# Up projection of the second MLP: three 256-column products per weight tile instead of one of 512 and one of 256 columns

## The chip, the cores and the metric

The kernel runs on one core of a Trainium2 chip. The metric is the device time of one execution in microseconds; the time quoted for a kernel is the median of its runs. A trace of one execution, taken by the hardware profiler, stands beside the times.

## The reference, cut to what matters

The reference is a two-layer trunk (a recurrent block beside windowed attention in the first layer, a state-space layer with a gated projection in the second), with a squared-ReLU MLP behind each layer. The sequence has 256 frames, the model 2048 channels, the hidden layer of an MLP 8192. The change touches the MLP of the second layer:

```python
h = rmsnorm(x, ffn_norm[layer])
x = x + jnp.square(jax.nn.relu(h @ w_up[layer])) @ w_down[layer]
```

All data is float32.

## The kernel before, in words

**Two parts of each number.** TensorE multiplies in fp32r, which keeps fewer bits than float32. The kernel therefore splits each operand into a high part (rounded to fp32r) and a low part (the rest, rounded again), and a product A·W is summed from three: high·high, low·high and high·low. For the up projection the normalized input stands in the tile `A1` with channels on the partitions: `A1[:, k, 0:L]` is the high part of channel block k (L = 256 frames) and `A1[:, k, L:2*L]` its low part. One product with the high part of a weight tile as the stationary operand and all 512 columns of `A1[:, k, :]` as the moving one gives A_high·W_high in columns 0 to 255 of a PSUM bank and A_low·W_high in columns 256 to 511; a second one, with the low part of the weight tile and the 256 columns of the high part of the input, adds A_high·W_low to columns 0 to 255. Every product instruction comes with a weight load of its own 128x128 stationary operand.

**Staging of the second MLP.** The hidden layer is done in 8 rounds (`NE`, index `e`) of 1024 hidden channels. A round has an up stage of 4 pairs (`NPAIR`, index `j`) of 128-channel output blocks (index `t`). A pair contracts 16 channel blocks, held in 4 weight slots (index `s`) of 4 blocks each (index `c`). That makes 8 x 4 x 4 x 2 x 4 = 1024 weight tiles of 128x128, one 512-column product (L1258) and one 256-column product (L1259) for each. A pair fills two of the four `ps` banks, and pairs take turns in them. Then a round multiplies its hidden channels with the down weights: in rounds 0 to 6 two plain blocks (`second_block`, L1270 to L1272) and two groups of seven products on sums of quadrants (`seven_products`, L1311 to L1313), in the last round four plain blocks; their products all have 512 columns. The order of the work is the order of each engine's program; semaphores link the engines.

**The weights' way.** A weight slot comes by DMA into `raws`, ScalarE rounds it to the high part (L1730), VectorE takes the difference as the low part (L2292), and TensorE frees the slot with `slot_used`. A ring of 7 slots serves up and down weights alike.

**After a pair.** ScalarE copies columns 256 to 511 of the two banks to `cross` (`up_cross`, L1753), VectorE adds columns 0 to 255 to it (L2338, which then frees the banks with `up_read`), and applies the ReLU and the frames' scale (L2340, `scaled_up`). ScalarE squares (L1759) and rounds (L1761), VectorE makes the low parts (L2352) and the sums of quadrants for the seven products. These steps stand between the slots' rounding steps at the fixed places 4j+9 to 4j+11 of a round's slots.

**Opening.** The first four weight tiles of some pairs (the first pair of rounds 1 to 7, the pairs 1 to 3 of round 0) are multiplied in another order by `opening` (L828 with 512 columns, L826 with 256), which the first MLP uses as well. In form 3 the widths follow as 512, 256, 512, 512, 256, 256, 512, 256.

Of the kernel before, what the change touches and what calls it, by code (L numbers as in the profile page):

```python
# [28 lines left out]
ACT = mybir.ActivationFunctionType  # L29
ALU = mybir.AluOpType  # L30
AX = mybir.AxisListType

P = 128
D = 2048
L = 256
KC = D // P
# [12 lines left out]
UK = 4  # L49
# [17 lines left out]
NE = 8  # L67
NPAIR = 4
# [9 lines left out]
E_SLOTS = S_SLOT + QUADS * NPR  # L78
# [76 lines left out]
def trunk_kernel(nc, x, mix_norm_e, w_in_e, conv_w, conv_b, lru_wa, lru_ba, lru_wx, lru_bx, lru_lambda,  # L155
# [4 lines left out]
    with ctx:  # L160
        def sb(name, shape, dt=F32, on=ctx):
            return on.enter_context(nc.sbuf_tensor(name, shape, dt))

        def sem(name):
            return ctx.enter_context(nc.semaphore(name))
# [10 lines left out]
        A1 = sb("A1", [P, KC, 2 * L], F32R)  # L176
# [12 lines left out]
        Wh = sb("Wh", [P, NU, UK, TW], F32R)  # L189
        with ExitStack() as o:  # L190
            Wt = sb("Wt", [P, NU, UK * TW], on=o)
        Wl = sb("Wl", [P, NU, UK, TW], F32R)
# [47 lines left out]
        cross = sb("cross", [P, 2, 2, L])  # L240
# [35 lines left out]
        ps = ctx.enter_context(nc.psum_tensor("ps", [P, 4, 512], F32))  # L276
# [113 lines left out]
        slot_lo = sem("slot_lo")  # L390
        slot_used = sem("slot_used")
        t_summed = sem("t_summed")
        up_crossed = sem("up_crossed")
        up_read = sem("up_read")
        hid_done = sem("hid_done")
        scaled_up = sem("scaled_up")
        sx_done = sem("sx_done")
        a_hi = sem("a_hi")
        s_hi = sem("s_hi")
        a_done = sem("a_done")  # L400
        s_done = sem("s_done")
# [70 lines left out]
        def out_unit(u):  # L472

            return (u // 4, NU + u % 4) if u < 4 * NU else (u // 4 - NU, u % 4)

        def out_banks(b):

            return ps[:, 2 - 2 * b:4 - 2 * b, :] if b < 2 else px[:, 2 * b - 4:2 * b - 2, :]
# [17 lines left out]
        def sum_bank(n):  # L496

            return px[:, 0 if n in (2, 3) else 3, 0:L]
# [5 lines left out]
        def wide(t, s):  # L504

            return t[:, s].rearrange("p (k a) n -> p k (a n)", k=2)
# [32 lines left out]
        def in_tiles(ap, n):  # L539

            return ap.rearrange("p (c n) -> p c n", n=n)
# [29 lines left out]
        def gain(col):  # L571

            return pcol[:, bass.ds(col, 1)]
# [184 lines left out]
        def _(pe):  # L758
            mm = nc.tensor.matmul
# [56 lines left out]
                    for u in range(NU, 2 * NU):  # L816
                        products(u, 1).then_inc(unit_done, 1)

            def opening(form, b, A, high=Wh[:, 0], low_=Wl[:, 0]):

                order = {1: ((0, 0), (0, 1), (1, 1), (1, 0), (2, 0), (2, 1), (3, 0), (3, 1)),
                         2: ((0, 0), (1, 0), (0, 1), (1, 1), (2, 0), (2, 1), (3, 0), (3, 1)),
                         3: ((0, 0), (0, 1), (1, 0), (2, 0), (1, 1), (2, 1), (3, 0), (3, 1))}[form]
                for c, low in order:
                    if low:
                        mm(ps[:, b, 0:L], low_[:, c, 0:P], A[:, c, 0:L], start=False, stop=False)  # L826
                    else:
                        mm(ps[:, b, :], high[:, c, 0:P], A[:, c, :], start=(c == 0), stop=False)  # L828

            def pair(g, d, A, ready=None, base=0, per_unit=0, turn=0, beside=None, freed=None, form=None):  # L830

# [57 lines left out]
            for a in range(2):  # L889
                last = mm(sum_bank(1)[:, bass.ts(a, P)], ones[:, :], sq[:, a, 0:P], start=True, stop=True)  # L890
# [124 lines left out]
            for u in range(8 * NU):  # L1015
                b, n = out_unit(u)
# [10 lines left out]
                for h in range(2):  # L1027
                    for c in range(2):
                        k = 2 * n + c
                        high = A2[:, k, h * P:h * P + P]  # L1030
                        low = A2[:, k, L + h * P:L + h * P + P]
                        to = out_banks(b)[:, h, :]
                        mm(to, high, wide(Wh, u % NU)[:, c], start=(k == LC), stop=False)
                        mm(to, high, wide(Wl, u % NU)[:, c], start=False, stop=False)
                        last = mm(to, low, wide(Wh, u % NU)[:, c], start=False, stop=(k == LC - 1))
# [129 lines left out]
            for h in range(2):  # L1165
                n = NC4 // 2
                last = mm(sum_bank(3)[:, h * n:h * n + n], pos4[:, :], sq[:, h, 0:n], start=True, stop=True)
# [61 lines left out]
            def last_block(s):  # L1229

                if s == 1:
                    turn_back(3, px, x_glu, 8)
                if s == 2:
                    frame_sum(4, 6)

            def second_up(e, j):

                b = 2 * (j % 2)
                if j >= 2:
                    pe.wait_ge(up_read, e * NPAIR + j - 1)  # L1240
                elif e:
                    pe.wait_ge(acc_read, (e - 1) * NPR + 2 * j + 2)
                else:
                    pe.wait_ge(pair_read, P_MLP1 - 4)
                form = 3 if e and j == 0 else j if e == 0 and 1 <= j <= 3 else None
                for s in range(NU):
                    p = e * E_SLOTS + j * UK + s
                    high, low = [in_tiles(v, TW) for v in slot_parts(p)[0:2]]
                    pe.wait_ge(slot_lo, p + 1)
                    if e == 0 and j == 0:  # L1250
                        pe.wait_ge(a1_ready, 16 + 2 * (s + 1))
                    if form and s == 0:
                        opening(form, b, A1, high, low)
                    for t in range(1 if form and s == 0 else 0, 2):
                        for c in range(UK):
                            k = s * UK + c
                            cols = slice(t * P, t * P + P)
                            mm(ps[:, b + t, :], high[:, c, cols], A1[:, k, :], start=(k == 0), stop=False)  # L1258
                            last = mm(ps[:, b + t, 0:L], low[:, c, cols], A1[:, k, 0:L], start=False, stop=(k == KC - 1))  # L1259
                    last.then_inc(slot_used, 1)  # L1260
                    if e == 0 and j == 0:
                        last_block(s)
# [67 lines left out]
        def _(act):  # L1330
            fn = nc.scalar.activation
# [65 lines left out]
            for i in range(KC // 2):  # L1397
                act.wait_ge(xt_done, i + 1)
                src = px[:, i % 3, :].rearrange("p (c t) -> p c t", c=2)
                for c in range(2):  # L1400
                    last = fn(A1[:, 2 * i + c, 0:L], src[:, c], ACT.Copy, scale=gain(G_MIX0 + 2 * i + c))
# [341 lines left out]
                    act.wait_ge(t_summed, (e * QUADS + Q) * 4 + i - T1 + 1)  # L1743
                    fn(to, in_tiles(slot_parts(p)[2], 512), ACT.Copy).then_inc(slot_hi, 1)

            def up_cross(e, j):

                d = j % 2
                act.wait_ge(slot_used, e * E_SLOTS + (j + 1) * UK)
                if e * NPAIR + j >= 2:  # L1750
                    act.wait_ge(a_done, e * NPAIR + j - 1)
                    act.wait_ge(s_done, min(e * NPAIR + j - 1, (NE - 1) * NPAIR))
                fn(cross[:, d], ps[:, 2 * d:2 * d + 2, L:2 * L], ACT.Copy).then_inc(up_crossed, 1)  # L1753

            def hidden_high(e, j):

                d = j % 2
                act.wait_ge(scaled_up, e * NPAIR + j + 1)
                fn(cross[:, d], cross[:, d], ACT.Square).then_inc(hid_done, 1)  # L1759
                act.wait_ge(hid_done, e * NPAIR + j + 1)  # L1760
                fn(blocks_of(0, 0, j), cross[:, d].rearrange("p c (h n) -> p (c h) n", h=2), ACT.Copy).then_inc(a_hi, 1)  # L1761
# [13 lines left out]
            def beside_slot(e, n):  # L1775

                if e == 0 and n == 4:
                    frame_squares(3, x_glu, 6, 1)
                    act.preload_act_table(ACT.Sqrt)
                if e == 0 and n == 5:  # L1780
                    operand_back(3, px, G_FF1, 16)
                if e == 0 and n == 6:
                    var.wait(act)
                    root.inc(fn(rs[:, :], nv[:, :], ACT.Sqrt))
                for j in range(NPAIR):
                    if n == 4 * j + 9:
                        up_cross(e, j)
                    if n == 4 * j + 10:
                        hidden_high(e, j)
                    if n == 4 * j + 11:  # L1790
                        sums_high(e, j)
                if e == 0 and n == E_SLOTS - 1:
                    first_product(0)
                if e == 1 and n < NPR - 1:
                    first_product(n + 1)
# [15 lines left out]
        def _(dve):  # L1811
            tt, ts, stt = nc.vector.tensor_tensor, nc.vector.tensor_scalar, nc.vector.scalar_tensor_tensor
# [40 lines left out]
            for i in range(KC // 2):  # L1853
                hi.wait(dve)
                src = px[:, i % 3, :].rearrange("p (c t) -> p c t", c=2)
                for c in range(2):
                    k = 2 * i + c
                    last = stt(A1[:, k, L:2 * L], src[:, c], gain(G_MIX0 + k), A1[:, k, 0:L].bitcast(F32),
                               ALU.mult, ALU.subtract)
# [23 lines left out]
            rs2 = rs[:, :].unsqueeze(1).to_broadcast([P, 2, L])  # L1883
# [188 lines left out]
            for g in range(P_XB, P_OUT):  # L2072
                j = g - P_XB
# [69 lines left out]
            for u in range(11, 36):  # L2143
                if u in (24, 28, 32):
                    b = (u - 24) // 4
# [188 lines left out]
            def hidden(e, j):  # L2334

                d = j % 2
                dve.wait_ge(up_crossed, e * NPAIR + j + 1)
                tt(cross[:, d], ps[:, 2 * d:2 * d + 2, 0:L], cross[:, d], ALU.add).then_inc(up_read, 1)  # L2338
                dve.wait_ge(up_read, e * NPAIR + j + 1)
                stt(cross[:, d], cross[:, d], 0.0, rs2, ALU.max, ALU.mult).then_inc(scaled_up, 1)  # L2340

            def hidden_low(e, j):

# [91 lines left out]
            e, at = NE - 1, (NE - 1) * E_SLOTS + C_SLOT  # L2435
# [388 lines left out]
```

## Time and profile before

| What | us |
|---|---|
| Median of 3 runs | 1981.22 |
| Range of the runs | 1980.56 to 1982.72 |
| The profiled execution, its own time | 1982.93 |
| Span of its trace, first to last instruction | 1981.0 |
| TensorE busy with products in the span | 1940.9 |
| VectorE busy | 1402.2 |
| ScalarE busy | 993.1 |

The span leaves out 1.93 us of the profiled execution's time, ahead of the first and behind the last instruction. Products overlap each other in the trace, as each is shown until its last result is written; how fast TensorE works is read from the distance between the starts of successive products.

### The profile page before, as it was taken

To read this page: it belongs to the slowest core of one execution; us is meant where nothing else is said; L and a number is where in the kernel's file an instruction comes from. 1 tells how busy PE (TensorE), PEld (TensorE's weight loads), DVE (VectorE), ACT (ScalarE), POOL (GpSimd) and SP (SyncE) were. 2 spreads that over 40 slices of the span, in tenths; PEclk is the share of its full clock that TensorE was granted. 3 is DMA by queue.
4 is the path that set the end of the run, shared out by engine and by line. 5 is a ranking of instruction groups with operands and counts; after the bars stand their busy time and mean duration, and the time that the engine had idled before them with its cause. 6 is when DMAs were issued, how large, how long until landed. Compare 5 with 4: busy or idle time off the path is not lost.

```text
span 1981.0 us, 30350 instructions
## 1 busy us (share of the span) xinstructions
PE 1940.9 (98%) x11494; PEld 1633.0 (82%) x11494; DVE 1402.2 (71%) x1613; ACT 993.1 (50%) x1331; POOL 650.2 (33%) x858
## 2 busy tenths in 40 slices
PE   8999999999999999999997999999999999999999
PEld 7888788888888888888876788888888878888887
DVE  6885768755765676566559655579798887979794
ACT  6467564433443444344452544556555555546452
POOL 3592439878687778440018300000000000000000
PEclk9999999999999999999999999999999999999999
DMA  7644576676666666686788666757373846647472
GB/s 226 182 138 139 178 194 203 201 230 209 210 204 226 210 203 232 208 264 199 250 279 290 186 190 189 235 182 231 127 256 111 274 146 216 203 137 252 131 254 87
DMA packets 278422, 400.25 MB, mean 202 GB/s; under 512 B 23328, under 2 KB 185264, under 8 KB 276240
## 3 DMA queue, kind: packets, MB, share of 16 engines
q1 hardware_dynamic: 270864, 371.77, 59.2%
q0 software_dynamic: 5216, 24.52, 4.0%
q10 hardware_dynamic: 2208, 2.11, 0.3%
q8 instruction: 92, 1.51, 0.3%
q14 instruction: 42, 0.34, 0.0%
HBM read 371.87 MB, written 25.17 MB: 200 GB/s over the span
## 4 chain that ended last, share of the span: by engine, by line
PE 84%; DVE 10%; issue 3%; ACT 2%; POOL 1%; DMA 1%; SPq 0%; DVEq 0%; ACTq 0%; POOLq 0%
PE ps L849 16%; PE ps L1258 12%; PE ps L850 8%; PE ps L801 6%; PE ps L803 6%; PE ps L802 6%; PE ps L1259 6%; PE px L1272 2%; PE px L1270 2%; PE px L1271 2%; DVE Vl L2292 2%; DVE Vt L2312 2%; PE px L1181 1%; PE px L1179 1%; PE px L1180 1%
## 5 line engine op out<-in xcount | busy, mean ns | idle before, releaser
L1827 DVE TENSOR_TENSOR Wl<-raw,Wh 128x1024 fp32r<-128x1024 f32 x404 | 531.1, 1324 | 371.2 <-ACT Wh L1346 369.9
L1346 ACT ACTIVATE Wh<-raw 128x1024 fp32r<-128x1024 f32 x404 | 423.3, 1058 | 449.8 <-PE ps L803 189.6
L849 PE MATMUL ps<-A,Wh 128*128 128x512 f32 x1364 | 480.6, 397 | 1.9 <-DVE A L1914 1.0
L850 PE MATMUL ps<-A,Wl 128*128 128x256 f32 x1364 | 379.5, 278 | 0.0
L849 PEld LDWEIGHTS ps<-A,Wh 128*128 128x128 f32 x1364 | 255.7, 187 | 63.1 <-issue 4.2
L850 PEld LDWEIGHTS ps<-A,Wl 128*128 128x128 f32 x1364 | 256.7, 188 | 0.2
L1258 PE MATMUL ps<-A,Vh 128*128 128x512 f32 x572 | 201.6, 396 | 0.0
L801 PE MATMUL ps<-Wh,A 128*128 128x512 f32 x512 | 200.6, 392 | 0.0
L803 PE MATMUL ps<-Wh,A 128*128 128x512 f32 x512 | 199.3, 389 | 0.0
L802 PE MATMUL ps<-Wl,A 128*128 128x512 f32 x512 | 199.3, 389 | 0.0
L2292 DVE TENSOR_TENSOR Vl<-raws,Vh 128x1024 fp32r<-128x1024 f32 x140 | 169.7, 1220 | 26.0 <-ACT Vh L1730 25.6
L1259 PE MATMUL ps<-A,Vl 128*128 128x256 f32 x572 | 159.6, 279 | 0.0
L1730 ACT ACTIVATE Vh<-raws 128x1024 fp32r<-128x1024 f32 x116 | 121.0, 1055 | 52.1 <-PE ps L1259 34.3
L1258 PEld LDWEIGHTS ps<-A,Vh 128*128 128x128 f32 x572 | 107.4, 188 | 25.9 <-issue 0.2
L801 PEld LDWEIGHTS ps<-Wh,A 128*128 128x128 f32 x512 | 96.1, 188 | 20.2
L803 PEld LDWEIGHTS ps<-Wh,A 128*128 128x128 f32 x512 | 96.1, 188 | 20.2
L802 PEld LDWEIGHTS ps<-Wl,A 128*128 128x128 f32 x512 | 96.1, 188 | 19.5
L1259 PEld LDWEIGHTS ps<-A,Vl 128*128 128x128 f32 x572 | 107.7, 188 | 0.0
L1258 PE MATMUL ps<-A,Wl 128*128 128x512 f32 x276 | 97.6, 396 | 0.0
L2292 DVE TENSOR_TENSOR Wl<-raws,Wl 128x1024 fp32r<-128x1024 f32 x68 | 82.7, 1220 | 12.6 <-ACT Wl L1730 12.4
L1259 PE MATMUL ps<-A,Wl 128*128 128x256 f32 x276 | 77.1, 279 | 0.0
L1597 ACT ACTIVATE A<-cross 128x512 fp32r<-128x512 f32 (+1 forms) x32 | 20.2, 632 | 106.4 <-DVE cross L2162 106.4
(520 smaller groups left out, 3948.2 us busy)
## 6 DMA issues: line engine op xcount, KB each, us to landing
raw<-in_w_up_dram SPq DMA_DIRECT2D x128, 512.0 KB, 4.1
raw<-in_w_down_dram SPq DMA_DIRECT2D x128, 512.0 KB, 4.3
raws<-in_w_up_dram SPq DMA_DIRECT2D x128, 512.0 KB, 6.2
raws<-in_w_down_dram SPq DMA_DIRECT2D x128, 512.0 KB, 4.4
raw<-in_w_glu_dram SPq DMA_DIRECT2D x64, 512.0 KB, 4.0
raw<-in_w_in_e_dram SPq DMA_DIRECT2D x52, 512.0 KB, 3.9
raw<-in_w_out_e_dram SPq DMA_DIRECT2D x32, 512.0 KB, 3.8
s_params<-stg POOLq DMA_DIRECT2D x16, 1024.0 KB, 5.9
```

The costliest lines, as they stand in the source:

```text
L801: mm(to, high, wide(Wh, u % NU)[:, c], start=(k == 0), stop=False)
L802: mm(to, high, wide(Wl, u % NU)[:, c], start=False, stop=False)
L803: last = mm(to, low, wide(Wh, u % NU)[:, c], start=False, stop=(k == KC - 1))
L849: mm(ps[:, b + t, :], Wh[:, s, c, cols], A[:, k, :], start=(n == 0), stop=False)
L850: last = mm(ps[:, b + t, 0:L], Wl[:, s, c, cols], A[:, k, 0:L], start=False, stop=(n == KC - 1))
L1258: mm(ps[:, b + t, :], high[:, c, cols], A1[:, k, :], start=(k == 0), stop=False)
L1259: last = mm(ps[:, b + t, 0:L], low[:, c, cols], A1[:, k, 0:L], start=False, stop=(k == KC - 1))
L1270: mm(to, stands(0, 2 * c + h, u), high[:, c], start=(u == 0 and c == 0), stop=False)
L1346: fn(Wh[:, s], raw[:, s], ACT.Copy).then_inc(hi_split, 1)
L1730: fn(slot_parts(p)[0], raws[:, r % NRAW], ACT.Copy).then_inc(slot_hi, 1)
L1827: tt(Wl[:, s], raw[:, s], Wh[:, s].bitcast(F32), ALU.subtract).then_inc(lo_split, 1)
L2292: tt(in_tiles(lo_part, n), of, in_tiles(hi_part, n).bitcast(F32), ALU.subtract).then_inc(slot_lo, 1)
```

## The change

Each weight tile of the second MLP's up projection is multiplied in three products of 256 columns: high weights with the high part of the input, low weights with the high part, high weights with the low part. All three are summed in columns 0 to 255 of the bank, and columns 256 to 511 stay unused. The ScalarE copy `up_cross` and the VectorE addition go; VectorE reads the sum straight from PSUM in its ReLU step. The second MLP no longer calls `opening`.

```diff
-                form = 3 if e and j == 0 else j if e == 0 and 1 <= j <= 3 else None
                 for s in range(NU):
...
-                    if form and s == 0:
-                        opening(form, b, A1, high, low)
-                    for t in range(1 if form and s == 0 else 0, 2):
+                    for t in range(2):
                         for c in range(UK):
                             k = s * UK + c
                             cols = slice(t * P, t * P + P)
-                            mm(ps[:, b + t, :], high[:, c, cols], A1[:, k, :], start=(k == 0), stop=False)
-                            last = mm(ps[:, b + t, 0:L], low[:, c, cols], A1[:, k, 0:L], start=False, stop=(k == KC - 1))
+                            to = ps[:, b + t, 0:L]
+                            mm(to, high[:, c, cols], A1[:, k, 0:L], start=(k == 0), stop=False)
+                            mm(to, low[:, c, cols], A1[:, k, 0:L], start=False, stop=False)
+                            last = mm(to, high[:, c, cols], A1[:, k, L:2 * L], start=False, stop=(k == KC - 1))
                     last.then_inc(slot_used, 1)
...
-            def up_cross(e, j):
+            def hidden_high(e, j):
 
                 d = j % 2
-                act.wait_ge(slot_used, e * E_SLOTS + (j + 1) * UK)
-                if e * NPAIR + j >= 2:
-                    act.wait_ge(a_done, e * NPAIR + j - 1)
-                    act.wait_ge(s_done, min(e * NPAIR + j - 1, (NE - 1) * NPAIR))
-                fn(cross[:, d], ps[:, 2 * d:2 * d + 2, L:2 * L], ACT.Copy).then_inc(up_crossed, 1)
-
-            def hidden_high(e, j):
-
-                d = j % 2
-                act.wait_ge(scaled_up, e * NPAIR + j + 1)
+                act.wait_ge(up_read, e * NPAIR + j + 1)
                 fn(cross[:, d], cross[:, d], ACT.Square).then_inc(hid_done, 1)
...
                 for j in range(NPAIR):
-                    if n == 4 * j + 9:
-                        up_cross(e, j)
                     if n == 4 * j + 10:
...
             def hidden(e, j):
 
                 d = j % 2
-                dve.wait_ge(up_crossed, e * NPAIR + j + 1)
-                tt(cross[:, d], ps[:, 2 * d:2 * d + 2, 0:L], cross[:, d], ALU.add).then_inc(up_read, 1)
-                dve.wait_ge(up_read, e * NPAIR + j + 1)
-                stt(cross[:, d], cross[:, d], 0.0, rs2, ALU.max, ALU.mult).then_inc(scaled_up, 1)
+                dve.wait_ge(slot_used, e * E_SLOTS + (j + 1) * UK)
+                stt(cross[:, d], ps[:, 2 * d:2 * d + 2, 0:L], 0.0, rs2, ALU.max, ALU.mult).then_inc(up_read, 1)
```

## Rows read from the trace of the kernel before

**Rows 1.** The page: span, busy time by engine, chain that ended last by engine.

```profile
span 1981.0 us, 30350 instructions
PE 1940.9 (98%) x11494; PEld 1633.0 (82%) x11494; DVE 1402.2 (71%) x1613; ACT 993.1 (50%) x1331; POOL 650.2 (33%) x858
PE 84%; DVE 10%; issue 3%; ACT 2%; POOL 1%; DMA 1%; SPq 0%; DVEq 0%; ACTq 0%; POOLq 0%
```

**Rows 2.** Up stages of rounds 1 to 7: PE, PEld, DVE, ACT, POOL busy; clock; DMA.

```profile
1361.94:1406.81 44.87, 44.87 (x258) 39.09 (x257) 35.49 (x42) 29.42 (x37) 0.00 (x0) 1.00 0.85 282
...
1713.14:1758.41 45.27, 45.27 (x256) 39.33 (x257) 37.67 (x47) 25.74 (x31) 0.00 (x0) 1.00 0.83 274
...
sum 314.83, PE 314.82 PEld 274.21 DVE 264.35 ACT 181.90 POOL 0.00; mean PE 44.97 PEld 39.17 DVE 37.76 ACT 25.99 POOL 0.00
```

**Rows 3.** All waits of TensorE, round 1 to round 2's start: us, times, longest.

```profile
PE px L1311 <- DVE Zl L2292: 0.6, 1, 0.6
PE ps L828 <- DVE acc L2375: 0.6, 1, 0.6
```

**Rows 4.** Timeline of TensorE, 48 tiles of round 6's up stage: start, duration.

```profile
1804.24 0.40 PE L1258 MATMUL ps<-A,Wl 128*128 128x512 f32 x1
1804.47 0.28 PE L1259 MATMUL ps<-A,Wl 128*128 128x256 f32 x1
...
1820.88 0.40 PE L1258 MATMUL ps<-A,Zh 128*128 128x512 f32 x1
```

**Rows 5.** Timeline of TensorE, 41 steps between 512-column products of a down block.

```profile
1408.65 0.39 PE L1272 MATMUL px<-Wl,A 128*128 128x512 f32 x1
...
1417.94 0.39 PE L1271 MATMUL px<-Vl,A 128*128 128x512 f32 x1
```

**Rows 6.** Timeline of TensorE, an opening of the first MLP.

```profile
661.93 0.39 PE L828 MATMUL ps<-A,Wh 128*128 128x512 f32 x1
662.16 0.28 PE L826 MATMUL ps<-A,Wl 128*128 128x256 f32 x1
662.27 0.63 PE L828 MATMUL ps<-A,Wh 128*128 128x512 f32 x2
662.74 0.39 PE L826 MATMUL ps<-A,Wl 128*128 128x256 f32 x2
662.97 0.40 PE L828 MATMUL ps<-A,Wh 128*128 128x512 f32 x1
...
663.32 0.39 PE L849 MATMUL ps<-A,Wh 128*128 128x512 f32 x1
```

**Rows 7.** Timeline of TensorE, three tiles of round 4's up stage.

```profile
1632.02 0.28 PE L1259 MATMUL ps<-A,Vl 128*128 128x256 f32 x1
...
1633.08 0.28 PE L1259 MATMUL ps<-A,Vl 128*128 128x256 f32 x1
```

**Rows 8.** Timeline of round 1's up stage, products and weight loads.

```profile
1376.81 0.19 PEld L1258 LDWEIGHTS ps<-A,Vh 128*128 128x128 f32 x1
1376.92 0.39 PE L1258 MATMUL ps<-A,Vh 128*128 128x512 f32 x1
1376.93 0.19 PEld L1259 LDWEIGHTS ps<-A,Vl 128*128 128x128 f32 x1
```

**Rows 9.** The chain of work, 32 small products of the state-space layer: start, us.

```profile
1072.26 1.08 PE px L1140 x32
```

**Rows 10.** The lines that change behind a pair: ns min/median/max of one.

```profile
L1753 ACT ACTIVATE cross<-ps x32: 574/598/601, 1288.0 to 1934.1; 128x512 f32<-128x512 f32 x32
L2338 DVE TENSOR_TENSOR cross<-ps,cross x32: 682/692/693, 1292.1 to 1934.7; 128x512 f32<-128x512 f32 x32
L2340 DVE SCALAR_TENSOR_TENSOR cross<-cross,rs x32: 691/692/694, 1292.9 to 1935.4; 128x512 f32<-128x512 f32 x32
```

**Rows 11.** Waits of VectorE, and the window of the seven products, in round 1.

```profile
DVE Vt L2312 <- PE px L1272: 5.9, 1, 5.9
1428.70:1449.59 20.89, 19.70 (x85) 15.42 (x83) 20.84 (x22) 12.85 (x13) 0.00 (x0) 1.00 0.43 137
```

More of the change, by code:

```diff
@@ L392, in trunk_kernel @@
         t_summed = sem("t_summed")
-        up_crossed = sem("up_crossed")
         up_read = sem("up_read")
         hid_done = sem("hid_done")
-        scaled_up = sem("scaled_up")
         sx_done = sem("sx_done")
@@ L817, in token_block, with opening @@
                         products(u, 1).then_inc(unit_done, 1)
-            def opening(form, b, A, high=Wh[:, 0], low_=Wl[:, 0]):
+            def opening(form, b, A):
                 order = {1: ((0, 0), (0, 1), (1, 1), (1, 0), (2, 0), (2, 1), (3, 0), (3, 1)),
@@ L825, in opening @@
                     if low:
-                        mm(ps[:, b, 0:L], low_[:, c, 0:P], A[:, c, 0:L], start=False, stop=False)
+                        mm(ps[:, b, 0:L], Wl[:, 0, c, 0:P], A[:, c, 0:L], start=False, stop=False)
                     else:
-                        mm(ps[:, b, :], high[:, c, 0:P], A[:, c, :], start=(c == 0), stop=False)
+                        mm(ps[:, b, :], Wh[:, 0, c, 0:P], A[:, c, :], start=(c == 0), stop=False)
             def pair(g, d, A, ready=None, base=0, per_unit=0, turn=0, beside=None, freed=None, form=None):
```

## The prediction, made before the kernel ran

> **What bounds the kernel now.** I read the page first: TensorE is busy 98% of the span and holds 84% of the chain that ended last [rows 1]. A busy share says little here, because products overlap in the record, so the next view is the one by windows over the up stages of the second MLP. In the seven stages of rounds 1 to 7 TensorE is busy for the whole 314.83 us, at a granted clock of 1.00 (the level of 2.4 GHz), with 256 products each [rows 2]. VectorE is busy 264 of these microseconds and ScalarE 182, so neither is the bound. The view of waits then says what TensorE stands still for. From the start of round 1 to the start of round 2 it lists two waits of 0.6 us: one inside the seven products, one at the first product of the next round; none ends with the steps behind a pair (ScalarE's copy, VectorE's addition) [rows 3]. The up stage is therefore a bare stream of products, and the change is worth what it does to the distance between their starts. That is read in the timeline.
>
> **The stream now.** From 1804.24 to 1820.88 there are 48 tiles in 16.64 us, 346.7 ns for a pair of one 512-column and one 256-column product [rows 4]. In a down block, with 512 columns only, 41 steps take 9.29 us, 226.6 ns each [rows 5]. At 2.4 GHz 512 columns are 213.3 ns, so 13.3 ns are added to each product; 768 columns are 320 ns, and the pair shows 26.7 ns more, which is 13.3 for each of its two. That reads as a fixed addition per product, whatever its width. The stage as a whole runs a little worse: 314.83 us over 7 x 128 tiles are 351.4 ns for a tile. Some stretches hold the slower rhythm of three tiles in 1.06 us, 353.3 ns [rows 7].
>
> **What the change adds: 1024 products, each with a weight load.** The trace has no run of three 256-column products, but it has two of them in succession, in the opening order 512, 256, 512, 512, 256, 256, 512, 256. Beside the alternating order that one has one step from 512 to 512 and one from 256 to 256 in place of one from 512 to 256 and one from 256 to 512. It takes 663.32 - 661.93 = 1.39 us [rows 6], and four alternating pairs take 4 x 346.7 ns = 1.387 us. So if a step depends on its two neighbours alone, a step from 256 to 256 is 346.7 - 226.6 = 120.1 ns, which is 106.7 ns of streaming plus the same 13.3 again. Single stamps scatter by more than that: the two 256-column products of the opening span 662.74 to 662.97, which alone reads as 115 ns each, but the steps around them are longer, so I take the sum over the whole order and not the two steps. Three products are then 360.3 ns, 13.6 ns more than the pair, and 1024 x 13.6 ns = +13.9 us.
>
> Bounds. Below: a step out of a 256-column product reads 0.11 us at its shortest [rows 6, 8], so three are 330 ns, -16.7 ns a tile or -17 us. Above, inside the same mechanism: the 4.7 ns by which the stage's tile exceeds the undisturbed pair (351.4 against 346.7) may vanish, which leaves 360.3 - 351.4 = 8.9 ns or +9.1 us, or grow with the number of products, by a half, which makes +16.3 us. I keep it as it is, the middle.
>
> Can TensorE feed the added instructions? In the state-space layer 32 small products, each with its load, start within 1.08 us, 34 ns for one [rows 9]. A product and a load every 120 ns are far from that.
>
> Are the added loads hidden? The load for a 256-column product begins at 1376.93, 0.01 us after the preceding product started, and the load for a 512-column one at 1376.81 is followed by that product at 1376.92, although the load is shown with 0.19 us [rows 8]. So a product can start 0.11 us after its load began, and the load lies under the product before it, even when that has only 256 columns. The Trainium skill ("TensorE: Matmul & The Clock Gate", Part 3, The mechanism) says that a weight load overlaps a matmul in flight only when its row group differs. All loads here take all 128 rows, and the trace disagrees by the two rows just named. By that rule each added load would stand by itself, which is the last rival below.
>
> **What the change removes.** ScalarE loses 32 copies of 598 ns, 19.1 us. VectorE loses 32 additions of 692 ns, 22.1 us; its ReLU step stays, now read from PSUM, where the addition shows that 512 columns cost the same 692 ns [rows 10]. I cost both at nothing: they lie under TensorE's stream, and the waits show no product that waited for them [rows 3]. If that cover were gone, only the last pair of a round could pass its gain on, at most 8 x 1.3 us = 10 us. VectorE does bound one stretch, the seven products (20.84 us busy in 20.89), but before it VectorE stands idle 5.9 us until a down block frees a weight slot [rows 11]. Time that it wins in the up stage ends in that idle time; the stretch starts when TensorE lets it. The banks come free 0.6 us earlier, and the next user of a bank comes a whole pair later, about 11 us (32 x 0.35). No DMA is moved or added: weight slots are freed by the last product of a slot as before, in an up stage that is longer by 1.7 us a round, so transfers get more time. The order of `opening` goes without effect, by the equality above.
>
> Sum, for the profiled execution: 1982.93 + 13.9 = 1996.8 us. The median of the runs stands 1.7 us below that execution, so the forecast is 1981.2 + 13.9 = 1995.1 us.
>
> **Rivals.**
> 1. The addition goes by columns, not by products (faster). 226.6 ns for 512 columns would be 113.3 for 256, three are 339.9, -6.8 ns a tile, -6.9 us: 1974.3 us; with 0.11 us steps 1964. For it: the steps out of 256-column products, 0.11 to 0.115 us as stamped. Against it: the alternating pair would be 339.9 as well, and shows 346.7; the change of width would have to cost the rest. It decides below 115.8 ns a product, where 1024 tiles lose 4.0 us.
> 2. A step keeps the length that it has in the alternating order (no change). The 512-column product is followed after 0.23 us [rows 4], which leaves 117 ns for the other one. Three are 350 ns, +3.5 us: 1984.7 us. For and against are as in the first; this is the same scatter of stamps, read more mildly. The Trainium skill ("TensorE: Matmul & The Clock Gate", Back-to-back issue gap) gives columns over 2.4 GHz plus about 2.5 ns for a gap. By it the third product would cost 2.5 ns, an estimate of +2.6 us or 1983.8. The trace disagrees in the size: its addition is 13.3 ns for 512 columns.
> 3. The loads are not hidden in an unbroken run of 256-column products (much slower). Each added load then costs up to the 0.19 us that it is shown with: 1024 x 0.19 = +195 us, 2176 us. Rows 8's load under a 256-column product speaks against it; for it only that there the next product was always a long one, under which the loads could catch up.
>
> **How the numbers follow.** A measurement of this kernel can tell about 0.2%, 4.0 us. I give the forecast 0.80 (its own range +9.1 to +16.3 us, 1990.3 to 1997.5), the first rival 0.09, the second 0.07, the third 0.04. Slower by over 0.2% is 0.80 + 0.04 = 0.84, within 0.2% is 0.07, faster 0.09. The range takes the forecast's own and reaches a few microseconds to either side, towards the second rival below and towards loads that show by some 4 ns above: 1987.5 to 2001.5 us.
>
> **What would show it.** In the changed kernel the up stages of rounds 1 to 7 should take 46.1 to 47.0 us each where they took 45.0, at a granted clock of 1.00, with 384 products; three products of a tile should start within 0.36 us of the next tile's three; the down blocks and seven products should take as long as before, with the same two waits; ScalarE's and VectorE's busy time should fall by about 19 and 22 us without effect on the end. Steps of 0.113 us in an unbroken run would prove the first rival, steps well over 0.12 us the third. A wait of TensorE for the ReLU step, or another length of the seven products, would mean that the stream is not all there is.

## The result, and the profile after

The changed kernel takes 1989.5 us (median of 6 runs, 1987.6 to 1991.7) against 1982.0 us of the kernel before (6 runs): ratio 1.0038, 95% interval 1.0025 to 1.0051. It is 7.6 us slower, in the forecast direction, inside the range, and a little over half of the +13.9 us of the sum. It lies also just below the forecast's own range, 1990.3 to 1997.5 us.

The page of the changed kernel, in the parts that answer to [rows 1]:

```profile
span 1987.8 us, 32304 instructions
PE 1951.9 (98%) x12518; PEld 1689.2 (85%) x12518; DVE 1386.1 (70%) x1581; ACT 979.3 (49%) x1299; POOL 650.0 (33%) x858
PE 83%; DVE 10%; issue 3%; ACT 2%; DMA 1%; POOL 1%; DVEq 0%; SPq 0%; ACTq 0%; POOLq 0%
```

1024 products and 1024 weight loads more, 32 instructions fewer on VectorE and on ScalarE. The span is 6.8 us longer. The view by windows of the up stages of rounds 1 to 7, first, longest and sum, with the columns of [rows 2]:

```profile
1362.84:1408.44 45.60, 45.60 (x386) 45.60 (x385) 33.79 (x39) 28.07 (x34) 0.00 (x0) 1.00 0.84 279
...
1806.13:1852.04 45.91, 45.91 (x385) 45.91 (x386) 36.03 (x44) 24.27 (x28) 0.00 (x0) 1.00 0.82 271
...
sum 320.78, PE 320.78 PEld 320.78 DVE 252.55 ACT 172.17 POOL 0.00; mean PE 45.83 PEld 45.83 DVE 36.08 ACT 24.60 POOL 0.00
```

Round 0 has such a stage too, here before and after the change:

```profile
1273.48:1319.80 46.32, 46.32 (x269) 40.42 (x268) 40.84 (x57) 30.98 (x43) 0.00 (x0) 1.00 0.77 251
```

```profile
1273.56:1320.69 47.13, 47.13 (x397) 47.12 (x396) 39.02 (x54) 29.75 (x40) 0.00 (x0) 1.00 0.77 250
```

The seven stages are 320.78 - 314.83 = 5.95 us longer and round 0's is 47.13 - 46.32 = 0.81 us longer, together 6.8 us, the whole difference of the spans. So the time went where the sum put it, into the stream of products; nothing else moved. A tile now takes 320.78 / 896 = 358.0 ns (896 is 7 stages of 128 tiles), where it took 351.4.

The reader should now look at the starts of the products themselves. The timeline of TensorE in round 1, where a slot in the fifth buffer of the weight ring (tiles `Zh`, `Zl`) is followed by one in another buffer (`Wl`):

```profile
1365.72 0.28 PE L1254 MATMUL ps<-A,Zh 128*128 128x256 f32 x1
1365.83 0.28 PE L1255 MATMUL ps<-A,Zl 128*128 128x256 f32 x1
1365.94 0.28 PE L1256 MATMUL ps<-A,Zh 128*128 128x256 f32 x1
...
1368.44 0.28 PE L1254 MATMUL ps<-A,Wl 128*128 128x256 f32 x1
1368.56 0.28 PE L1255 MATMUL ps<-A,Wl 128*128 128x256 f32 x1
1368.68 0.28 PE L1256 MATMUL ps<-A,Wl 128*128 128x256 f32 x1
...
1369.64 0.28 PE L1255 MATMUL ps<-A,Wl 128*128 128x256 f32 x1
```

In the `Wl` slot ten steps take 1.20 us, 120 ns each: the forecast step. In the `Zh` slot 24 steps take 1368.44 - 1365.72 = 2.72 us, 113.3 ns each. Of the 16 slots of the fifth buffer in rounds 1 to 7, 14 take 2.72 us; the other two (2.93 and 2.82 us) are the first two of round 6, which starts with this buffer, and whose stage is the longest above. The kernel before had no step length that belonged to a buffer in any row shown, and the forecast knew nothing of it.

What TensorE waits for, from round 1 to the start of round 2, and VectorE's ReLU step and its idle time ahead of the seven products:

```profile
PE px L1308 <- DVE Zl L2278: 0.6, 1, 0.6
PE ps L1254 <- DVE acc L2359: 0.6, 1, 0.6
```

```profile
1408.64 0.69 DVE L2324 SCALAR_TENSOR_TENSOR cross<-ps,rs 128x512 f32<-128x512 f32 x1 [0.34 <-PE ps L1256]
...
1422.36 1.22 DVE L2298 TENSOR_TENSOR Vt<-raws 128x1024 f32<-128x1024 f32 x1 [5.94 <-PE px L1269]
```

These are the same two waits as in [rows 3]. The ReLU step still takes 0.69 us, now from PSUM [rows 10], and VectorE still stands idle 5.9 us for a down block before the seven products [rows 11].

### The profile page after: what moved, and what is told of

Read it like the earlier page. It is cut to its first block, busy times and chain, and to the rows that moved or that the text cites. A ratio compares the mean times of both kernels' runs of the same rounds, so it can differ in the third digit from the quotient of the medians.

```text
span 1987.8 us, 32304 instructions
## 1 busy us (share of the span) xinstructions
PE 1951.9 (98%) x12518; PEld 1689.2 (85%) x12518; DVE 1386.1 (70%) x1581; ACT 979.3 (49%) x1299; POOL 650.0 (33%) x858
## 4 chain that ended last, share of the span: by engine, by line
PE 83%; DVE 10%; issue 3%; ACT 2%; DMA 1%; POOL 1%; DVEq 0%; SPq 0%; ACTq 0%; POOLq 0%
PE ps L847 16%; PE ps L848 8%; PE ps L1254 6%; PE ps L1256 6%; PE ps L1255 6%; PE ps L799 6%; PE ps L801 6%; PE ps L800 6%; PE px L1267 2%; PE px L1268 2%; PE px L1269 2%; DVE Vl L2278 2%; DVE Vt L2298 2%; PE px L1179 1%; PE px L1178 1%
## 5 line engine op out<-in xcount | busy, mean ns | idle before, releaser
L848 PE MATMUL ps<-A,Wl 128*128 128x256 f32 x1364 | 379.9, 279 | 0.0
L1254 PE MATMUL ps<-A,Vh 128*128 128x256 f32 x592 | 168.0, 284 | 1.7 <-DVE acc L2359 1.7
L1255 PE MATMUL ps<-A,Vl 128*128 128x256 f32 x592 | 167.5, 283 | 0.0
L1256 PE MATMUL ps<-A,Vh 128*128 128x256 f32 x592 | 167.5, 283 | 0.0
L1254 PEld LDWEIGHTS ps<-A,Vh 128*128 128x128 f32 x592 | 113.5, 192 | 3.2 <-DVE acc L2359 3.0
L1255 PEld LDWEIGHTS ps<-A,Vl 128*128 128x128 f32 x592 | 113.5, 192 | 0.0
L1256 PEld LDWEIGHTS ps<-A,Vh 128*128 128x128 f32 x592 | 113.5, 192 | 0.0
L1254 PE MATMUL ps<-A,Wl 128*128 128x256 f32 x288 | 81.7, 284 | 1.1 <-DVE acc L2359 1.1
```

The source lines that it names most:

```text
L848: last = mm(ps[:, b + t, 0:L], Wl[:, s, c, cols], A[:, k, 0:L], start=False, stop=(n == KC - 1))
L1254: mm(to, high[:, c, cols], A1[:, k, 0:L], start=(k == 0), stop=False)
L1255: mm(to, low[:, c, cols], A1[:, k, 0:L], start=False, stop=False)
L1256: last = mm(to, high[:, c, cols], A1[:, k, L:2 * L], start=False, stop=(k == KC - 1))
```

## The experiments

The theory after the result: each 256-column product costs a step of its own, 120 ns, or 113 ns in the fifth buffer; the shorter way behind a pair is worth nothing. The main rival: the products cost the full +13.9 us, and the work taken from ScalarE and VectorE gave half of it back.

### The products alone

```diff
-                            last = mm(to, high[:, c, cols], A1[:, k, L:2 * L], start=False, stop=(k == KC - 1))
+                            last = mm(ps[:, b + t, L:2 * L], high[:, c, cols], A1[:, k, L:2 * L], start=False, stop=(k == KC - 1))
```

against the changed kernel, with `up_cross` and the addition in `hidden` as before the change.

> The three 256-column products stay, but the third one goes to columns 256 to 511 again, so that ScalarE's copy and VectorE's addition stay as before the change. Theory (the products alone make the difference, ScalarE's and VectorE's saving is hidden): up stages of rounds 1 to 7 as in the changed kernel, 45.6 to 45.9 us each, and +7 to +8 us against the kernel before, 1989 to 1990 us. Rival (the products cost the +13.9 us of the forecast and the shorter way behind a pair gave back half of it): up stages or waits behind them longer than in the changed kernel, 1995 us or more.

Measured: 1989.0 us, ratio to the kernel before 1.0035 (1.0023 to 1.0047), the same as the changed kernel. The windows of its seven up stages, sum:

```profile
sum 320.68, PE 320.68 PEld 320.68 DVE 264.41 ACT 182.28 POOL 0.00; mean PE 45.81 PEld 45.81 DVE 37.77 ACT 26.04 POOL 0.00
```

VectorE is busy 12 us and ScalarE 10 us more than in the changed kernel, in a stage of the same length. Whether the three products share their columns is without effect too. The rival falls.

### The shorter way behind a pair alone

```diff
-                tt(cross[:, d], ps[:, 2 * d:2 * d + 2, 0:L], cross[:, d], ALU.add).then_inc(up_read, 1)
-                dve.wait_ge(up_read, e * NPAIR + j + 1)
-                stt(cross[:, d], cross[:, d], 0.0, rs2, ALU.max, ALU.mult).then_inc(scaled_up, 1)
+                stt(cross[:, d], ps[:, 2 * d:2 * d + 2, 0:L], 0.0, rs2, ALU.max, ALU.mult).then_inc(up_read, 1)
```

and no `up_cross`, on the products of the kernel before.

> The products of the kernel before (512 and 256 columns, with the opening), but behind a pair ScalarE's copy and VectorE's addition are left out: the low part of the input times the high part of the weights is computed and not added. Theory: no difference to the kernel before, within 2 us of 1982, with ScalarE busy about 19 us less and VectorE 22 us less. Rival (the shorter way behind a pair is worth something by itself): 6 to 7 us faster, about 1975 us.

Measured: 1981.5 us, ratio 0.9999 (0.9990 to 1.0008). The saving is hidden, as forecast. Its page shows what is saved:

```profile
PE 1941.7 (98%) x11494; PEld 1633.5 (83%) x11494; DVE 1383.6 (70%) x1581; ACT 979.5 (49%) x1299; POOL 647.7 (33%) x858
```

ScalarE is busy 13.6 us less and VectorE 18.6, not 19.1 and 22.1. The instructions are shown longer than the distance to the next one: in the kernel before a copy starts at 1407.01, is shown with 0.60 us, and ScalarE's next instruction starts at 1407.51.

### A fourth product

```diff
-                            last = mm(to, high[:, c, cols], A1[:, k, L:2 * L], start=False, stop=(k == KC - 1))
+                            mm(to, high[:, c, cols], A1[:, k, L:2 * L], start=False, stop=False)
+                            last = mm(to, low[:, c, cols], A1[:, k, L:2 * L], start=False, stop=(k == KC - 1))
```

> The changed kernel with a fourth 256-column product for each tile, low part of the input times low part of the weights, into the same columns (a term that the reference's value has and the kernels leave out). Theory (each 256-column product costs its own step of 120 ns, 113 ns in the fifth buffer, and nothing else): 1024 x 119 ns = +122 us against the changed kernel, 2111 us, tiles of 480 ns. Rival (weight loads catch up under other work, so that more of them in a row cost more): tiles longer than 490 ns, over 2122 us.

Measured: 2110.9 us (2 runs), +121.4 us against the changed kernel. The seven up stages, sum:

```profile
sum 427.39, PE 427.38 PEld 427.39 DVE 254.94 ACT 171.82 POOL 0.00; mean PE 61.05 PEld 61.06 DVE 36.42 ACT 24.55 POOL 0.00
```

(427.39 - 320.78) / 896 = 119.0 ns for the fourth product, (320.78 / 896) / 3 = 119.3 for each of the first three. The price does not grow with the number of products and loads in a row: no load shows.

### Without the opening

```diff
-                form = 3 if e and j == 0 else j if e == 0 and 1 <= j <= 3 else None
+                form = None
```

> The kernel before, only without the opening order in the second MLP. Theory (a step depends on its two neighbours alone): no difference in the first slot of a pair, the time within 2 us of 1982. Rival (the opening order sets off the slower rhythm of 353 ns a tile that half of the slots of the kernel before show): all slots but those of the fifth buffer at 2.77 us, about 3.7 us faster, 1978 us.

Measured: 1985.4 us (11 runs, 1980.6 to 1986.1), ratio 1.0011 (1.0002 to 1.0020). Both expectations miss: it is not faster, and its median is 3.3 us above that of the kernel before, where within 2 us was expected. In its trace the seven up stages sum to this:

```profile
sum 315.33, PE 315.33 PEld 274.46 DVE 264.34 ACT 181.82 POOL 0.00; mean PE 45.05 PEld 39.21 DVE 37.76 ACT 25.97 POOL 0.00
```

That is 0.5 us more than before the change. The slower rhythm stays without the opening, so it does not need the opening. The trace belongs to the fastest of its runs; where most of the others have 4 to 5 us more stays open, as no trace of them is on record.

### The fifth buffer

The buffers' starts are worked out from the order and the sizes of the tiles in the source; no trace shows an address. By them the input tile, the second operand tile and six of the seven weight buffers start on a multiple of 128 bytes in a partition, the fifth buffer 64 bytes off one. In rounds 1, 2, 3, 6 and 7 of the kernel before, the slower rhythm (that of [rows 7]) sets in at the second slot of the fifth buffer in the round. The timeline of TensorE in round 1, first product of such a slot, of its third tile and of the next slot:

```profile
1384.20 0.40 PE L1258 MATMUL ps<-A,Zh 128*128 128x512 f32 x1
...
1384.91 0.39 PE L1258 MATMUL ps<-A,Zh 128*128 128x512 f32 x1
...
1387.03 0.39 PE L1258 MATMUL ps<-A,Wl 128*128 128x512 f32 x1
```

Eight tiles take 2.83 us, 354 ns each, where 346.7 is the undisturbed pair. The buffer is not the only place where the rhythm begins: in rounds 4 and 5 it stands from the round's first slots. [rows 7], at 1632.02, is of round 4, whose first slot of the fifth buffer starts 10 us later:

```profile
1642.02 0.39 PE L1258 MATMUL ps<-A,Zh 128*128 128x512 f32 x1
```

Two kernels move the buffer onto a multiple of 128, one from the changed kernel and one from the kernel before:

```diff
+        pad0 = sb("pad0", [P, 16])
         with ExitStack() as o:
             cti = sb("cti", [P, 2, TPC, HD + 2 * SH], on=o)
...
         slot_last = sb("slot_last", [P, S_ALL])
+        pad1 = sb("pad1", [P, 48])
```

> The changed kernel with the fifth weight buffer moved by 64 bytes in each partition (a pad ahead of it and one behind), so that it starts on a multiple of 128 bytes as the other six buffers and the input do. Theory (a step is 113 ns instead of 120 where the stationary operand starts 64 bytes off a multiple of 128): the slots of this buffer go from 2.72 to 2.88 us, the up stages of rounds 1 to 7 to 46.1 to 46.3 us; as moving operand in the down blocks the buffer loses what it costs there, some 1 to 2 us; together within 2 us of the changed kernel. Rival (the buffer is quicker for its far place in the memory or for what ScalarE and VectorE do in its turn): its slots stay at 2.72 us.

> The kernel before with the same move of the fifth weight buffer. Theory (the slower rhythm of 353 ns a tile in the kernel before starts in slots of that buffer, because of where it lies): all slots but the first of a round take 2.77 us, up stages of 44.4 to 44.5 us instead of 44.7 to 45.3, 3.5 us less in all, and 1 to 2 us less in the down blocks: 1976 to 1978 us, faster than both kernels. Rival (the rhythm has another cause): slower slots as before, 1980 to 1982 us.

Measured on one chip, beside the same runs of the kernel before (1982.3 us): from the changed kernel 1992.4 us, ratio 1.0053 (1.0038 to 1.0069); from the kernel before 1978.5 us, ratio 0.9983 (0.9974 to 0.9992). The slot of the fifth buffer in the first, its first product and that of the next slot, and the seven stages:

```profile
1362.77 0.28 PE L1256 MATMUL ps<-A,Zh 128*128 128x256 f32 x1
...
1365.64 0.28 PE L1256 MATMUL ps<-A,Wl 128*128 128x256 f32 x1
```

```profile
sum 323.11, PE 323.11 PEld 323.11 DVE 252.79 ACT 172.03 POOL 0.00; mean PE 46.16 PEld 46.16 DVE 36.11 ACT 24.58 POOL 0.00
```

and the stages of the second, longest and sum:

```profile
1447.02:1491.52 44.50, 44.50 (x256) 38.91 (x257) 37.66 (x47) 25.62 (x31) 0.00 (x0) 1.00 0.85 280
...
sum 311.38, PE 311.38 PEld 272.28 DVE 264.28 ACT 181.66 POOL 0.00; mean PE 44.48 PEld 38.90 DVE 37.75 ACT 25.95 POOL 0.00
```

In the first kernel the slot now takes 2.87 us instead of 2.72, so its shorter step came with where it lay, and not with its turn. The time is 2.9 us above the changed kernel's median, where within 2 us was expected; its own four runs spread over 5 us. In the second kernel no stage of these seven exceeds 44.50 us, where they went up to 45.27: the slower rhythm is gone from them. Four traces have these products with the buffer in its old place (the kernel before, without the copy and addition, without the opening, and with `A2` moved, below); none of their 28 stages of rounds 1 to 7 is under 44.68 us. The rhythm still stands in the last four slots of round 0, which are of other buffers and begin with an opening. Eight tiles of one of them take 2.83 us:

```profile
1312.14 0.40 PE L1260 MATMUL ps<-A,Vh 128*128 128x512 f32 x1
...
1314.97 0.40 PE L1260 MATMUL ps<-A,Vh 128*128 128x512 f32 x1
```

So in rounds 1 to 7 the rhythm came with the buffer's place, but that place is not all that can set it off. The kernel before with a pad is the only version tried that is faster than both kernels by more than the noise, by some 4 and 11 us.

### Other tiles moved by 64 bytes

Three more kernels ask how far the start of a tile decides: the four weight buffers that lie side by side (`Vh`, `Vl`, in the changed kernel), the stationary operand of the down blocks and most other 512-column products (`A2`, in the kernel before), and the input tile, the moving operand of the up stages (`A1`, in the changed kernel with the fifth buffer on a multiple of 128).

```diff
+            pad0 = sb("pad0", [P, 16], on=o)
             Vh = sb("Vh", [P, 4, UK * TW], F32R, on=o)
```

for the first; the two others have the same pad ahead of `A2` or of `A1`, and one of 192 bytes behind it, so that the tiles behind keep their starts modulo 128.

> The changed kernel with the four buffers of the weight ring that lie side by side moved by 64 bytes, so that five of seven are off a multiple of 128 and two on it. Theory: their slots in the up stages go from 2.88 to 2.72 us, about 73 slots, -11.7 us; as moving operands in the down blocks and the seven products their products go from 227 to 233 ns, about +5 us: 1982 to 1984 us. Rival (place or turn): no slot changes, 1989 us.

> The kernel before with the tile that is the stationary operand of the down blocks, the seven products and most 512-column products (the second operand tile) moved by 64 bytes. Theory in its simplest form (a load from an address 64 bytes off a multiple of 128 adds 6.7 ns less to its product, whatever the width): 512-column steps of these stages go from 226.7 to 220 ns, several thousand of them, 20 us or more faster. Rival (the gain is there only with 256-column products, where a step is nearly as short as a load): 512-column steps stay at 226.7 ns, within 3 us of the kernel before.

> The changed kernel with the fifth buffer on a multiple of 128 bytes and, in its place, the input tile (the moving operand of the up stages) moved by 64 bytes. Theory (it is the start of the stationary operand that makes 113 ns of 120): steps of the up stages are 120 ns or more, 46.1 us a stage or longer. Rival (it is the distance between the two operands, modulo 128 bytes): all slots at 2.72 us, stages of 43.6 us, 18 us less in the up stages.

Measured: 1987.6 us (ratio 1.0028, 1.0016 to 1.0040), 2003.1 us (1.0104, 1.0088 to 1.0119), and, in a single execution each, 1988.9 us beside 1984.8 for the kernel before. All three expectations miss. With the four buffers moved, the timeline shows a slot of the fifth buffer behind a moved one, and later a moved one behind one that was not:

```profile
1364.28 0.28 PE L1255 MATMUL ps<-A,Zh 128*128 128x256 f32 x1
...
1367.00 0.28 PE L1255 MATMUL ps<-A,Wl 128*128 128x256 f32 x1
...
1372.76 0.28 PE L1255 MATMUL ps<-A,Vh 128*128 128x256 f32 x1
...
1375.59 0.28 PE L1255 MATMUL ps<-A,Vh 128*128 128x256 f32 x1
```

2.72 us for the first, 113.3 ns a step, and 2.83 us for the second, 117.9 ns. The fifth buffer itself, which has not moved here, takes 2.72 us in this slot and 2.83 us in the two later ones of the same round. With `A2` moved, 39 steps between 512-column products of a down block take 9.11 us:

```profile
1425.28 0.40 PE L1272 MATMUL px<-Wl,A 128*128 128x512 f32 x1
...
1434.39 0.39 PE L1272 MATMUL px<-Vh,A 128*128 128x512 f32 x1
```

233.6 ns instead of 226.6: the opposite of what was expected, and 21 us in all. Some 18 of them arise ahead of round 0, where `A2` is the stationary operand of further 512-column products: round 0 starts at 1291.7 us, and at 1273.5 in the kernel before. With the input moved, a slot takes 2.83 us:

```profile
1371.89 0.28 PE L1258 MATMUL ps<-A,Wl 128*128 128x256 f32 x1
...
1374.72 0.28 PE L1258 MATMUL ps<-A,Wl 128*128 128x256 f32 x1
```

117.9 ns a step, neither 120 nor 113. The span of its trace, 1987.1 us, gains nothing on the 1986.6 us with the fifth buffer alone moved, as round 0 starts at 1277.4 us here, and between 1270.4 and 1274.1 in the traces with `A1` and `A2` in place: the input tile is an operand of earlier stages too. So where the operands start does decide by some nanoseconds, in steps of 113, 118 and 120 ns for 256 columns and 227 and 233 for 512; but it does not decide alone, as the same buffer takes 113 and 118 ns in one round, and no rule for it was found.

## Why the prediction was right, and where its size was off

**The step from 256 to 256 columns.** Right in size, with some luck. 120.1 ns were worked out from the opening; in rounds 1 to 7 the changed kernel shows 120 ns in every buffer that lies as the first MLP's weights do, but for the first slot of a round. The luck: [rows 6] is read to 0.01 us, which leaves a step worked out from it open by some 10 ns, so that this row alone could not tell 120 from 113. And the premise, that a step depends on its two neighbours alone, does not hold: the same succession of widths takes 113.3, 117.9 or 120 ns by where the tiles lie and by the slot. Rivals 1 and 2 (113.3 by columns, 117 by the alternating stamps) fall as accounts of the whole stream: with the fifth buffer on a multiple of 128 in both kernels, the stages of rounds 1 to 7 differ by 323.11 - 311.38 = 11.7 us and round 0's by 47.46 - 46.30 = 1.2 us, together 12.9 us, 12.6 ns a tile where 13.6 were forecast. The medians differ by 1992.4 - 1978.5 = 13.9 us, but the runs of each kernel spread over 5 to 6 us, so that this fits more closely than it can be read. The step of 113 ns that rival 1 asked for does occur, but in one buffer, and goes when the buffer is moved. (Rival 1's price counts from 346.7 ns a tile, its threshold of 115.8 ns from 351.4; from 346.7 it is 114.3.) The Trainium skill ("TensorE: Matmul & The Clock Gate", Back-to-back issue gap) would leave 2.5 ns beyond the columns' own time; it gives this for a product by itself, and for a stream of loads and products about 131 ns at 512 columns. The traces disagree with both: 120 ns for 106.7 of streaming at 256 columns, and 226.6 ns at 512.

**The loads.** Right: hidden. Three in a row, and four in a row, cost 119 ns a product with its load. Rival 3 falls. The traces disagree with the sentence of the Trainium skill ("TensorE: Matmul & The Clock Gate", Part 3, The mechanism) that a load overlaps only a product of another row group: no load of this stream has another. The same section also lets a load for the background weight buffer go ahead of products; which buffer a load fills, no trace here shows.

**What was removed.** Right: nothing on the path, shown in both directions by the two halves of the change. Its size off the path was read too large, 19 and 22 us for 14 and 19 (measured alone). That the opening can go without effect is shown to a few microseconds only: without it the stages of the trace are 0.5 us longer, but the median of the runs is 3.3 us higher, and the cause of that is not shown.

**The sum.** The term that was mis-sized is the 4.7 ns by which a tile of the stage exceeded the undisturbed pair. The forecast kept it as it was, with bounds of none and half as much again: 351.4 + 13.6 = 365.0 ns a tile and stages of 46.1 to 47.0 us. Measured are 358.0 ns, 2.3 less than three steps of 120.1, and stages of 45.60 to 45.91 us. For the most part the excess was no general disturbance: it came, in rounds 1 to 7, with the alternation of widths together with the place of the fifth buffer. In the kernel before, that place cost (314.83 - 311.38) + (46.32 - 46.30) = 3.5 us, in the changed one it gives back (323.11 - 320.78) + (47.46 - 47.13) = 2.7 us. Taken from the 12.9 us above, the two leave 6.8 us (before rounding), as they must, since all are differences of the same stages. The first of the two was inside the bounds, as an excess that may vanish; the second, a buffer in which the new products are quicker, was not, and took the result below the forecast's own range.

## What to carry to other kernels

In a stream of products that TensorE never leaves, count products and not columns alone: here each costs 13.3 ns beyond its columns where all operands lie on multiples of 128 bytes (6.7 in most slots of the fifth buffer), so one of 512 columns is cheaper than two of 256, and work saved on other engines pays nothing. The price of a step that the trace does not hold can be estimated from two orders of the same products that take the same time, as closely as the stamps are read. An excess over the undisturbed step should be traced to the tile that it belongs to before it is carried over to other shapes; a list of slot times by buffer would have shown ahead of the run where the slower rhythm begins in most rounds, though not that the new products would be quicker in that buffer.

## What the runs showed of the hardware that was not expected

The place of a tile within a partition can change the step of a product: moving one weight buffer by 64 bytes made its 256-column steps 120 ns instead of 113.3, and moving the stationary tile of the 512-column products by 64 bytes made their steps 233.6 ns instead of 226.6. Alternating widths, 512 and 256, fall into one of two rhythms, 346.7 or about 353 ns a pair, and can stay in the slower one over many slots; with the buffer moved, the stages of rounds 1 to 7 kept the quicker one, while the end of round 0 did not. What in the chip makes these steps stays open.
